# A delta-rule layer's triangular inverse: 32x32 blocks on GpSimd and two doubling levels on TensorE, in place of 16x16 blocks and three

## What is computed

```
q, k, v = silu(causal_conv4(h @ w_in));  q, k unit length;  g = cumsum(log decay);  beta = sigmoid(...)
decay[i,j] = exp(g[i] - g[j])  for i >= j, else 0
lower      = strictly_lower((k*beta) @ k.T * decay)
u, w       = solve(I + lower, [v*beta, k*beta*exp(g)])
qk         = (q @ k.T) * decay
per chunk:  v_new = u - w @ S;  o = (q*exp(g)) @ S + qk @ v_new;  S = S*exp(g_last) + (k*exp(g_last-g)).T @ v_new
out        = rms_norm(o) * silu(z) @ w_out
```

## Time and profile before

| what | value |
|---|---|
| median of 3 runs | 2478.45 us (2476.84 to 2479.12) |
| the profiled execution's own time, its span | 2480.48 us, 2478.7 us |
| busy: PE, DVE, ACT, POOL | 95%, 57%, 51%, 9% |
| layer 0 stretch 540 to 660 us: PE, DVE, ACT, POOL busy | 116.47, 75.29, 69.39, 21.64 of 120 us |
| GpSimd waits for the loaded blocks (L565) | 316.3 us in 8 waits |
| 16 projection matmuls (slots 0 and 1 of head 5), first and last start | 597.61 and 601.15 us |
| PE starts head 0 to its last projection of head 7 | 60.01 to 935.6 us |

### The profile page before, as it was taken

The page is one execution under the profiler, slowest core; times in us unless marked ns, Lnnn a source line. Parts: engine busy times, 40 slices in busy tenths (PEclk is TensorE's granted clock), DMA queues, the critical chain, the costliest instruction groups (busy, mean ns, idle before and its releaser), DMA issues. The chain is left out here.

```text
span 2478.7 us, 35640 instructions
## 1 busy us (share of the span) xinstructions
PE 2360.4 (95%) x11614; PEld 1961.2 (79%) x11614; DVE 1422.6 (57%) x2614; ACT 1255.3 (51%) x2548; POOL 232.2 (9%) x387
## 2 busy tenths in 40 slices
PE   6999999999999997799699999999999999999979
PEld 5778888887878886688588888888888888888867
DVE  4746666575757563776472745637273654737245
ACT  4546555564656563445454545455454445455433
POOL 1021220202020211730000000000000000000000
PEclk9999999999999998899899999999999999999979
DMA  3021222203021211788311211111121211111067
GB/s 113 26 63 49 52 53 57 76 24 84 27 72 37 64 40 32 246 276 279 123 35 35 68 35 51 37 44 38 43 59 34 60 34 47 38 51 42 18 225 267
DMA packets 280353, 189.43 MB, mean 76 GB/s; under 512 B 72173, under 2 KB 258693, under 8 KB 280229
## 3 DMA queue, kind: packets, MB, share of 16 engines
q1 hardware_dynamic: 280228, 187.88, 25.7%
HBM read 160.38 MB, written 27.46 MB: 76 GB/s over the span
## 5 line engine op out<-in xcount | busy, mean ns | idle before, releaser
L336 PE MATMUL b_proj<-g_h_hi,wb_w_hi 128*128 128x512 f32 x1280 | 510.2, 399 | 5.0 <-PEq L234 5.0
L336 PE MATMUL b_proj<-g_h_lo,wb_w_hi 128*128 128x512 f32 x1280 | 511.5, 400 | 1.1
L336 PE MATMUL b_proj<-g_h_hi,wb_w_lo 128*128 128x512 f32 x1280 | 511.9, 400 | 0.0
L336 PE MATMUL a_proj<-g_h_hi,wa_w_hi 128*128 128x512 f32 x784 | 324.7, 414 | 8.1 <-PEq L234 6.1
L336 PE MATMUL a_proj<-g_h_lo,wa_w_hi 128*128 128x512 f32 x784 | 323.7, 413 | 0.0
L336 PE MATMUL a_proj<-g_h_hi,wa_w_lo 128*128 128x512 f32 x784 | 317.4, 405 | 0.0
L336 PEld LDWEIGHTS b_proj<-g_h_hi,wb_w_hi 128*128 128x128 f32 x1280 | 241.6, 189 | 54.9 <-issue 5.2
L336 PEld LDWEIGHTS b_proj<-g_h_lo,wb_w_hi 128*128 128x128 f32 x1280 | 241.8, 189 | 51.5 <-issue 1.8
L336 PEld LDWEIGHTS b_proj<-g_h_hi,wb_w_lo 128*128 128x128 f32 x1280 | 241.5, 189 | 49.1
L1528 ACT ACTIVATE b_acc<-b_proj,g_gains 128x512 f32<-128x512 f32 x96 | 66.1, 688 | 326.8 <-DVE b_qk L1785 193.9
L336 PEld LDWEIGHTS a_proj<-g_h_hi,wa_w_hi 128*128 128x128 f32 x784 | 149.3, 190 | 39.1 <-issue 7.0
(11 more groups left out here) (229 smaller groups left out, 4242.2 us busy)
## 6 DMA issues: line engine op xcount, KB each, us to landing
wb_raw<-in_b_w_in_dram SPq DMA_DIRECT2D x80, 512.0 KB, 3.9
p_w_raw<-in_a_w_out_dram SPq DMA_DIRECT2D x64, 512.0 KB, 3.8
wa_raw<-in_a_w_in_dram SPq DMA_DIRECT2D x48, 512.0 KB, 4.2
p_w_raw<-in_b_w_out_dram SPq DMA_DIRECT2D x32, 512.0 KB, 4.0
a_out<-a_og SPq DMA_DIRECT2D x64, 128.0 KB, 1.8
p_a_raw<-a_out SPq DMA_DIRECT2D x64, 128.0 KB, 4.6
a_zx<-inverse_tiles SPq DMA_DIRECT2D x16, 384.0 KB, 4.4
u_tiles<-a_u SPq DMA_DIRECT2D x8, 512.0 KB, 3.2
```

The lines of the kernel that those rows point to most:

```text
L336: last = pe.matmul(out, w[:, k, :], a[:, k, ks], start=(n == 0), stop=(n == 23))
```

## The change

Blocks are 32x32 (8 tiles x 4 blocks = 32 partitions, 31 steps), levels are two. `gram` takes k.k of four tiles at slots 11 and 14 and q.k at 17 and 20. Decay rows come from DRAM by one broadcast DMA a head, and DVE's L1031 reads them in place, at slots 8 and 11. `u` goes out at slot 16; its off-diagonal parts are loaded straight into `um` at slot 24 by three DMAs (GpSimd's mask product is gone). The inverse is stored and loaded back at slot 34 of the same body; levels begin at slot 0, the chain at slot 4. `z` has one buffer. `constants` makes no level masks.

```diff
-BLK = 16
+BLK = 32
-LEVELS = 3
+LEVELS = 2
-LEVEL0 = 1
-DECAYS = (12, 15)
-CHAIN0 = 7
+LEVEL0 = 0
+DECAYS = (8, 11)
+CHAIN0 = 4
-GRAM0 = 19
-BLOCKS_OUT = GRAM0 + T + 1
+GRAMS = (11, 14, 17, 20)
+BLOCKS_OUT = 16
+BLOCKS_ACROSS = 24
+BLOCKS_BACK = 34
...
-        z = m_.sb("z", [P, 2, VT, S])
+        z = m_.sb("z", [P, VT, S])
-        um = m_.sb("um", [P, 2, LEVELS, P])
+        um = m_.sb("um", [P, T, LEVELS, P])
...
+            def decays(n):
+                rows = cum_dram.rearrange("(t h) i -> t (h i)", h=H)[:, bass.ds(n * P, P)]
+                sp.dma_start(dec[:, :, :], rows.partition_broadcast(P)).then_inc(dec_in, 16)
...
                     if n is not None and s == BLOCKS_OUT:
+                        if not (isinstance(n, int) and n == 0):
+                            sp.wait_ge(um_in, n * 48)
-                        sp.wait_ge(ut, n * (T // 2) + T // 2)
+                        sp.wait_ge(ut, n * 4 + 2)
                         sp.dma_start(as_tiles(u_dram), u[:, :, :]).then_inc(blocks_out, 16)
...
+                    if n is not None and s == BLOCKS_ACROSS:
+                        sp.wait_ge(lv_s, n * (LEVELS * T // 2) + 1)
+                        tiles = as_tiles(u_dram)
+                        for j, i, level in ((slice(0, 32), slice(32, 64), 0), (slice(64, 96), slice(96, P), 0),
+                                            (slice(0, 64), slice(64, P), 1)):
+                            sp.dma_start(um[j, :, level, i], tiles[j, :, i]).then_inc(um_in, 16)
+                        if not (isinstance(n, int) and n == H - 1):
+                            sp.wait_ge(ut, n * 4 + 4)
+                            sp.sem_inc(carrier, 1)
+                            decays(n + 1)
+                    if n is not None and s == BLOCKS_BACK:
+                        sp.wait_ge(blocks_inv, n * 2 + 2)
...
-                    for b in range(T // 2):
-                        pool.wait_ge(first_mm, m * (LEVELS * T // 2) + (LEVELS * b + 1))
-                        pool.wait_ge(ut, m * (T // 2) + (b + 1))
-                        pool.tensor_tensor(um[:, :, :, :], spread(u[:, 2 * b:2 * b + 2, :], 2, LEVELS),
-                                           spread(g.level_mask[:, :, :], 1, 2), ALU.mult).then_inc(um_s, 1)
...
-                            for t in range(TH):
-                                last = pe.matmul(gram[:, t * P:(t + 1) * P], spread(hc[:, p, C_LOG, half * TH + t], 1, P),
-                                                 g.tri[:, :], start=True, stop=True)
...
+                        if s in GRAMS:
+                            c, half = divmod(GRAMS.index(s), 2)
+                            pe.wait_ge(kqn, n * 4 + (2 * c + half + 1))
+                            for e in range(TH):
+                                t = half * TH + e
+                                last = pe.matmul(gram[:, e * P:(e + 1) * P], kq[:, p, t, 0], kq[:, p, t, c, :],
+                                                 start=True, stop=True)
```

More of the change, by code:

```diff
@@ L138, in _ @@
             keep(g.decay_mask[:, :], [[1, P]], 0, -1, ALU.is_ge, -BIG)
[L140 to L148, removed]
             pool.memset(g.band_mask[:, :], 0.0).then_inc(zero, 1)
-            pool.wait_ge(zero, 6)
+            pool.wait_ge(zero, 4)
             keep(g.band_mask[:, 0:P], [[1, P]], 0, -1, ALU.is_ge, -BIG)
@@ L487, in _ @@
             sp.wait_ge(inv_zero, 32)
+            def decays(n):
+                rows = cum_dram.rearrange("(t h) i -> t (h i)", h=H)[:, bass.ds(n * P, P)]
+                sp.dma_start(dec[:, :, :], rows.partition_broadcast(P)).then_inc(dec_in, 16)
             def body(m, n, p):
                 for s in range(DELAYED):
[L491 to L501, removed]
+                    if m is None and s == 6:
+                        sp.wait_ge(totals, 3)
+                        sp.dma_start(cum_dram, cum_rows).then_inc(dec_in, 16)
+                        sp.wait_ge(dec_in, 16)
+                        decays(n)
                     if n is not None and s < SLOTS and s % 6 == 3:
@@ L745, in body @@
                 for s in range(SLOTS):
+                    if m is None and s == 3:
+                        pe.wait_ge(setup, 14)
+                        pe.transpose(turn[0:T * H, 0:P], cols[:, C_CUM].rearrange("p t h -> p (t h)"),
+                                     g.ident[:, :]).then_inc(totals, 1)
                     if m is not None:
@@ L855, in body @@
                                         pe.wait_ge(back[b], m * 32 + 32)
-                                    pe.wait_ge(um_s, m * (T // 2) + (b + 1))
+                                    if b == 0:
+                                        pe.wait_ge(um_in, m * 48 + 48)
                                 for e in range(2):
-                                    last = pe.matmul(first[:, e, :], um[:, e, level], x[:, e, 1], start=True, stop=True)
+                                    last = pe.matmul(first[:, e, :], um[:, 2 * b + e, level], x[:, e, 1], start=True, stop=True)
                                 last.then_inc(first_mm, 1)
@@ new lines, in body @@
+                        if s - 1 in GRAMS:
+                            c, half = divmod(GRAMS.index(s - 1), 2)
+                            tiles = slice(half * TH, (half + 1) * TH)
+                            dve.wait_ge(gram_mm, n * 4 + (2 * c + half + 1))
+                            if c == 0:
+                                dve.wait_ge(dexp, n * 2 + (half + 1))
+                                if not (isinstance(n, int) and n == 0):
+                                    dve.wait_ge(blocks_out, n * 16)
+                                for e in range(TH):
+                                    t = half * TH + e
+                                    ins = dve.scalar_tensor_tensor(u[:, t], gram[:, e * P:(e + 1) * P],
+                                                                   hc[:, p, C_BETA, t:t + 1], dec[:, t],
+                                                                   ALU.mult, ALU.mult)
+                                ins.then_inc(ut, 1)
+                            else:
+                                dve.tensor_tensor(attn[:, p, tiles], gram[:, :].rearrange("p (t i) -> p t i", t=TH),
+                                                  dec[:, tiles], ALU.mult).then_inc(ut, 1)
@@ L1025, in body @@
                         if s in DECAYS:
                             half = DECAYS.index(s)
-                            dve.wait_ge(row_mm, n * 2 + (half + 1))
+                            if not half:
+                                dve.wait_ge(dec_in, n * 16 + 32)
                             for t in range(TH):
                                 at = half * TH + t
-                                dve.scalar_tensor_tensor(dec[:, at], gram[:, t * P:(t + 1) * P],
+                                dve.scalar_tensor_tensor(dec[:, at], dec[:, at],
```

88 lines of the change are left out of this document (31 added, 57 removed).

## The result

The changed kernel takes 2465.82 us (median of 5 runs, 2464.89 to 2466.38), the kernel before 2478.45 (5 runs beside it): ratio 0.9949, 95% interval 0.9934 to 0.9963. It is 12.6 us faster, where 30 us slower was forecast. The profiled execution took 2465.82 us with a span of 2464.1, so the two spans differ by 14.6 us.

| stretch | before, us | after, us | change | forecast |
|---|---|---|---|---|
| span's start to head 0 | 60.0 | 56.1 | -3.9 | -1.5 |
| head 0 to the first resume | 89.1 | 102.9 | +13.8 | +14 |
| seven periods, resume to resume | 790.9 | 771.4 | -19.5 | +22 |
| last resume to the output projection | 69.0 | 63.7 | -5.3 | -4.5 |
| the rest | 1469.7 | 1469.9 | +0.2 | 0 |

What follows compares the result with a forecast made beforehand. The loop through GpSimd and DRAM was to bind: 113.9 us plus 2.2 for the clock, 116.1 a head against 113.0. Seven heads +22, first resume +14, ends -4.5 and -1.5: +30, 2508 us; range 2445 to 2552.

Steps and rivals of the forecast that it cites:

- The frame: Per head: loop from resume (PE's first level-0 matmul) over `u`, GpSimd and DRAM, 113.9 us, against PE's own 105.
- both ends (first resume, tail): First resume (PE's first level-0 matmul, head 0) +14 us, PE waiting some 20; last body, one level less, -4.5 us.
- the inversion: GpSimd's part of the loop, first product to transposed copy: 53 us a head, bounds 42 and 61.
- the exclusion: SBUF-only operations of DVE and GpSimd exclude each other; 28 of DVE's cost GpSimd 13 us a head, bounds 6 and 20.
- The operations alone: GpSimd's 62 inversion operations 33.6 us, gaps of 0.07 us (4.3 in all), transposing copy 2 to 3; undisturbed 40 us.
- the loop's four other terms: Resume to `u` 48.4 us, `u` to blocks 6.1, GpSimd's end to SP 0.3, SP to resume 6.1.
- the second rival: Exclusion bites harder: GpSimd 58 to 61 us, DVE waits 10 us a head; 2548 to 2572 us; chance 0.10.
- the clock's share: PE at granted clock 0.50 after its 9 us wait at the resume: 2.2 us a head between resume and `u`.
- what was to show it: 256-element subtraction near 0.7 us, operations lengthened beside taps, inversion 50 to 57 us, PE idle 8 to 11 (head 0: 20).
- The first rival, on the other side: GpSimd's inversion takes 42 to 48 us: 2452 us at 46, 2421 at 43; turning point 49; chance 0.27.
- The broadcast "at nothing": New transfers, including the 512 KB decay broadcast at slot 24, cost nothing: needed only next body, ten slots cover them.
- DVE bounding the head "speaks little": DVE waits for GpSimd 10 us a head in the second rival; little suggests DVE then bounds the head, busy 63%.

Runs made afterwards that it cites:

- pad16: The changed kernel with GpSimd clearing one element 16 times between the last subtraction and the transposing copy: 2496.39 us, ratio 1.006 to the kernel before.
- grams_late: The changed kernel with gram steps at slots 17, 20, 23, 26, `u` stored at 22, transfers across at 28: 2592.0 us, ratio 1.045 to the kernel before.
- tiny_split: The changed kernel with GpSimd's inversion on one element a partition and the decay broadcast in four pieces: 2414.01 us.
- few_taps: The changed kernel with the broadcast in four pieces and the second to fourth convolution taps on one column of 512: 2444.67 us.
- split_lean: The changed kernel with the broadcast in four pieces, DVE's negated copy of acc and the clamp at 44 left out: 2464.05 us, ratio 0.9932 to the kernel before.
- split: The changed kernel with the 512 KB decay broadcast cut into four, at slots 24, 28, 31 and 33: 2456.93 us, ratio 0.9905 to the kernel before.
- tiny_pool: The changed kernel with GpSimd's 62 products and subtractions on one element a partition and its transposing copy on one row: 2436.66 us.
- split_kd: The changed kernel with the broadcast in four pieces and `kd` made between the second and third tap: 2470.37 us, ratio 0.997 to the kernel before.

## Why the prediction was wrong

The frame was the right one: a loop through GpSimd against PE's own need. `pad16` and `grams_late` show that a longer loop sets the period, `tiny_split` that PE alone needs 105.2, and the table at the top that both ends (first resume, tail) were right. But in the changed kernel the loop binds only in heads 1, 2 and 7; in the others PE's program with its waits is the longer one.

**The term that failed is the inversion: 53 us where 47.0 were measured, and in it the exclusion, 13 us where 7.2 were.** The operations alone came as forecast (32.7 for 33.6, a copy of 2.13, gaps of 0.08), and the loop's four other terms lie within 0.4 us where nothing disturbs them (up to 7.3 for 6.1 from the inverse's store to the resume). The step was "each costs GpSimd its length less about 0.2 to 0.3". It took two collisions of a short operation for the rule. What `few_taps` measured is 0.32 us for a tap of 0.75 that follows another at once, and `split_lean` nothing that stands out of the noise for a copy of 0.43. The rows of the changed kernel tell why: the ends alternate at about 0.5 us, so what one engine keeps the other from is some 0.5 us, not the 0.75 or 0.68 of its record, and the rest of a record, with the gap behind it, falls into the other's turn. One operation of each takes 560.06 to 561.14, 1.08 us; GpSimd alone needs 0.68 + 0.07, so it pays 0.3, and DVE pays as much for its 0.75. DVE's part was priced at nothing but in the second rival. The Trainium skill (SBUF — State Buffer, SBUF: two separate sides) has it as an exclusive lock: whichever of the two starts first keeps the pair of ports for its whole instruction and the other is blocked. The trace agrees with the turns, and puts a turn at 0.5 us, shorter than the record of the instruction.

With 7.2 in place of 13 the forecast's own sum is 30 - 8 x 5.8 = -16 us without the clock's share touched, and about -32 with that gone too, as the wait that caused it was to be 3 us. That -16 lies near the measured -14.6 of the spans is luck: the clock's share, the waits at slots 23 and 27 and ACT's stall happen to fill the 16 us between.

Of what was to show it, the 256-element subtraction came at 0.73 us (0.7 forecast), operations beside the taps were lengthened, and the wait at head 0's resume was 14 us (some 20 forecast); but the inversion took under 49 us, which the prediction named as what would make it wrong.

**The first rival, on the other side, is what happened**, at 47 us, two under its turning point of 49. Its price (46 us: 2452) was too low by what follows.

**The broadcast "at nothing" was wrong.** "Ten slots cover them" looked at the one who needs the data; behind it in the queue stood the store of an output tile, whose buffer DVE needs back three slots on. The Trainium skill (DMA: Bandwidth & Descriptors, Queues, rings and completion order) says that on each DMA engine descriptors are taken in the order of the ring, and the trace agrees: the store took 8.6 to 9.4 us in place of 1.9. That made up to 1.4 us of the wait at slot 27, and with the half clock behind it `split` gives 11 us.

**DVE bounding the head "speaks little"** held for the head, not for slot 23, where `kd` stands behind a round of stretched taps: 2.0 us a head, GpSimd's by `tiny_pool` (16.4 to 2.9 us in all).

**The clock's 2.2 us a head** came, but not where they were put. Behind the resume, whose waits were 1.8 us at most from head 1 on, there was no half clock but for the stall; there it came in `split_kd` (resume to `u` 50 to 51.4 us for 48.5), and after the 14 us wait that ends head 0's loop. In the changed kernel 3.4 us of it stand behind slot 27 of heads 3 to 6 and slot 23 of heads 1 and 7, which by half the rate is up to 1.7 us each. The stall at the loop's jump, 6 us once, I had not foreseen.

## What to carry to other kernels

Price a transfer by what stands behind it in the queue, not only by when its own data is needed: a big one with slack is better issued in pieces. When a loop and an engine's own program are about equally long, taking waits out of the program only gathers them at the loop's end, and one long idle stretch can cost more than the same time in parts. That a longer loop lengthens the kernel doesn't show that the loop was what bound it before: look at each resume whether there was a wait. A price taken from two collisions needs the spread of many, above all when the sum multiplies it by 28.

## What was new about the hardware

- GpSimd and DVE took strict turns of about 0.5 us where DVE's taps met GpSimd's products and subtractions (ends at 560.06, 560.59, 561.14, 561.61, 562.16), and both pay: 0.32 us to GpSimd for each of DVE's taps, 0.25 to 0.3 to DVE for each tap beside GpSimd (829 ns the mean of all for 752). Six copies of 0.43 us cost GpSimd 0.3 us in all, about the noise.
- A broadcast of 512 KB in rows of 512 bytes took 9.3 us to land, a weight load of the same size 5.7; cut in four, a piece took 3.9. The store of an output tile right behind the whole took 8.6 to 9.4 us, behind the first piece 2.8 to 3.9; the median of all is 1.9.
- An idle stretch of PE of 3.9 us was followed by some 3.5 us at a granted clock of 0.50. In the changed kernel so were the seven waits of 2.2 to 2.9 us at slots 23 and 27, and none of the eight shorter ones there; in `split` two of three waits of 2.2 us were. Eight matmuls that nobody reads, put into such a wait, made a kernel 10 us faster.
- An engine (ACT, in `split_lean` DVE) can stand still at a loop's jump for up to 5.0 us (`few_taps`) with its data there; transfers ran at 310 GB/s just before. With less traffic there ACT's part was smaller in two pairs of runs.
